# A hybrid decoder step on one Trainium2 core: x kept in a place of its own, rows broadcast in one pass, and the opening's loads and chunk quarters dealt anew

## The chip, the cores and the metric

The kernel runs on one core of one Trainium2 chip. The metric is device time of one execution in microseconds (us), lower is better. The core has a matrix engine (PE, TensorE), a vector engine (DVE, VectorE), an activation engine (ACT, ScalarE), a general engine (POOL, GpSimd) and a queue engine (SP, SyncE) that here does nothing but ask for loads. All of them run their own instruction lists in parallel and meet only at semaphores.

## What is computed

One step of a one-layer decoder trunk in float32, for a prompt of 256 tokens and for 8 sequences of 4 tokens, 288 token columns in all. Cut to what matters here:

```python
mod = silu(c) @ ada_w + ada_b                    # 9 conditioning rows, ada_w is 2048 x 12288
sh1, sc1, g1, sh2, sc2, g2 = split(mod, 6)
h = rms_norm(x) * (1 + sc1) + sh1
proj = h @ w_in                                  # 2048 x 18448, then HGRN2 and mLSTM heads
x = x + g1 * (merged @ w_out)
h = rms_norm(x) * (1 + sc2) + sh2
up = h @ w_up;  x = x + g2 * ((gelu(conv(a)) * g) @ w_down)
y = rms_norm(x, final_norm_w)
```

The mLSTM heads (8 of them) need, for each head, one row of running values (`-m_t`, exponents and so on) under every one of 128 partitions: a broadcast.

## The kernel before

Every large product is made from "chunks": a chunk is 512 rows by 256 columns of a weight matrix, loaded as 512 KB into a ring of four buffers `raw`. ACT rounds it to a high part `whi` (helper `hi(N, k)`), DVE makes the low part `wlo = raw - whi` (helper `lo(N, k)`), and PE then makes 24 matmuls of 288 columns (`whi` by the high part of h, `whi` by its low part, `wlo` by the high part; lines L770 to L772, in `pieces`). A quarter of a chunk, 6 matmuls, is called a piece. 584 chunks pass through the kernel.

The opening is different from the rest. h cannot be made before the first 4096 columns of `mod` are known, and these come from 32 MB of `ada_w`. They are made by eight "units" (`unit(u, tiles)` on PE), each of four halves h; a half is two loads of 512 KB and 8 matmuls of 512 columns (L903). When a unit's four halves are done, ACT copies the sums out (`unit(u)` on ACT, to `urows`), PE turns them (`unit_turn(u)`), and DVE adds the groups. Each two units give four more rows of h. So that PE has work between the halves, the first 18 chunks (`EARLY`), each of which needs only a part of h, are dealt among the halves of units 2 to 7: 8 pieces before unit 2, then `EARLY_PIECES[4 * (u - 2) + h]` pieces behind half h of unit u, and the remaining pieces, up to 72, behind unit 7. The sums of chunks 0 to 5 are copied to `SQ` by ACT (`to_padded`), those of later chunks are added by DVE (`early_add`); either frees one of two accumulator banks, which the chunk two later needs.

ACT and DVE walk through the same deal. Behind half h of unit u come the chunks that end there:

```python
for n in chunk_ends(u, h):
    early_chunk(n)      # evict or add chunk n, then hi / lo of chunk n + 4
```

and on ACT `unit(u)`, the copy of unit u's sums, stands ahead of the chunks of half 3. The order is fixed when the program is built; nothing is chosen at run time.

SP asks for loads in one fixed order: the eight loads of a unit, and between them chunks 4 and up, as many as `loads_ahead(u, c)` says ahead of load c of unit u. A unit's load waits until the same half of the unit before is used (`u_used`); a chunk's load waits for `lo_done` of the chunk four earlier. What is left of the first 20 chunks is asked for behind unit 7's last load.

x, turned to columns (`xT`), lies at the start of the memory that `SQ` takes later. Before the first sums may be copied to `SQ`, POOL writes `xT` to DRAM (`xT_spill`, 2 writes of 1152 KB), waits for that, and clears the padding columns of `SQ` (`hg["pad"]`).

The mLSTM broadcast is one matmul per head, `mm(R[:, 0, 0:EM + TS], ones8[:, :], mLR[:, :])`, of a float32 block of 8 rows by 360 columns; `rows_of(h)` on DVE fills `mLR` from `LR`, keeping row h alone. The gate rows of the mLSTM (`gate_rows`) are made on ACT and DVE beside the chunks 18 to 25, from q = 18 (`EARLY`) on.

Of the kernel before, what the change touches and what calls it, by code (L numbers as in the profile page):

```python
# [174 lines left out]
EARLY_PIECES = (1, 2, 1, 2, 2, 2, 1, 2, 2, 1, 3, 3, 3, 3, 3, 3, 3, 3, 3, 3, 3, 2, 2, 2)  # L175
# [84 lines left out]
def build(nc, x_prompt, x_sample, c_prompt, c_sample, state_hgrn, state_mlstm_C, state_mlstm_n, state_mlstm_m,  # L260
# [5 lines left out]
    with ExitStack() as ctx:  # L266
# [54 lines left out]
        ones8 = sb("ones8", [MH, P], stack=mixer)  # L321
# [21 lines left out]
        ctm = sb("ctm", [P, 2, P], stack=setup)  # L343
        cvr = sb("cvr", [2 * FT, NS, P], stack=setup)
        partm = sb("partm", [P, 4, P], stack=setup)
# [6 lines left out]
        ssx = sb("ssx", [P, 3], stack=setup)  # L352
# [33 lines left out]
        mLR = sb("mLR", [MH, EM + TS], stack=ml_mem)  # L386
# [358 lines left out]
        def _(pe):  # L745
# [499 lines left out]
        def _(act):  # L1245
# [434 lines left out]
        def _(dve):  # L1680
# [123 lines left out]
            def early_chunk(n):  # L1804
# [3 lines left out]
                if n + RING < EARLY + LEAD:  # L1808
                    lo(N_HG, n + RING)
# [365 lines left out]
        def _(pool):  # L2175
# [14 lines left out]
            cst_(nc.gpsimd.memset(ones8[:, :], 1.0))  # L2190
# [34 lines left out]
            pool.dma_start(cvr[:, :, :], state_conv[0].rearrange("b j (t c) -> (j t) b c", c=P)).then_inc(ld_conv, 16)  # L2225
            pool.wait_ge(x_c, KT + X_FREE)
            pool.wait_ge(u_used, 4 * BESIDE)
            for half in range(2):
                pool.dma_start(xT_spill[:, half * KT * T // 2:(half + 1) * KT * T // 2],
                               xT[:, 8 * half:8 * half + 8, :].rearrange("p a b -> p (a b)")).then_inc(ml["st"], 16)  # L2230

            pool.wait_ge(ml["st"], 32)
            pool.wait_ge(xn_done, 4)
            nc.gpsimd.memset(SQ[:, :, :, TP:TPAD].rearrange("p a b t -> p (a b) t"), 0.0).then_inc(hg["pad"], 1)
            pool.wait_ge(u_used, 4 * UNITS - 1)
            with nc.allow_non_contiguous_dma(reason="a few columns"):
# [243 lines left out]
```

## Time and profile before

| | |
|---|---|
| three runs, us | 2230.81, 2230.97 (median), 2234.35 |
| the profiled execution, its time | 2232.91 us |
| its span in the profile | 2231.2 us |
| PE busy | 2179.2 us, 98% of the span |
| DVE, ACT, POOL busy | 1143.9, 984.5, 362.1 us |
| DMA | 460.03 MB moved |

The profile gives, for each engine, when each instruction started, how long it took, and for idle time ahead of it what it waited for. Matmul records overlap, since the engine is pipelined: the time from one start to the next says what a matmul costs, not the length of its record. Times inside the kernel are counted from the start of the span.

### The profile page before, as it was taken

The page shows a single profiled execution, that of the slowest core. Times are in us where ns is not written, and L with a number is a line of the kernel's source. Part 1 is how long each engine was busy: PE and PEld are TensorE (multiplying, and loading weights), DVE is VectorE, ACT ScalarE, POOL GpSimd, SP SyncE. Part 2 cuts the span into 40 slices and gives each one's busy share as a digit, 9 for nine tenths or more (in the row PEclk, how much of TensorE's full clock was granted, in tenths as well). Part 3 has the DMA queues.
Part 4 walks back from the last instruction along what each step waited for, and adds up shares of the span by engine and source line. Part 5 has one row for each costly group of instructions (what it writes and reads, how often), then busy time and mean ns, then how long its engine had stood idle before and what let it go on. Part 6 is the DMA issues. An engine that isn't in the chain of part 4 may idle for free. (4 is left out here: it accounts for less than half of the span.)

```text
span 2231.2 us, 42202 instructions
## 1 busy us (share of the span) xinstructions
PE 2179.2 (98%) x17218; PEld 2057.1 (92%) x17218; DVE 1143.9 (51%) x1597; ACT 984.5 (44%) x1365; POOL 362.1 (16%) x525
## 2 busy tenths in 40 slices
PE   6899999999999999999999998999999999999997
PEld 3589999999999999999999987999999999999997
DVE  3356465564565544444445466555555555444443
ACT  3336563564454344454535335434444444433332
POOL 2000322332222331121212240000000000110000
PEclk9999999999999999999999999999999999999999
DMA  9987666666675767668676698555555555555553
GB/s 351 376 283 216 203 197 206 209 199 211 208 226 188 235 190 233 197 211 257 210 222 202 200 311 266 163 167 163 166 167 159 170 161 161 181 161 174 173 168 106
DMA packets 407411, 460.03 MB, mean 206 GB/s; under 512 B 14843, under 2 KB 379955, under 8 KB 406433
## 3 DMA queue, kind: packets, MB, share of 16 engines
q1 hardware_dynamic: 394192, 410.64, 58.8%
q0 software_dynamic: 12240, 46.03, 6.4%
q8 instruction: 109, 1.79, 0.3%
q10 hardware_dynamic: 833, 1.26, 0.2%
q14 instruction: 37, 0.30, 0.0%
HBM read 431.48 MB, written 26.39 MB: 205 GB/s over the span
## 5 line engine op out<-in xcount | busy, mean ns | idle before, releaser
L770 PE MATMUL ps<-xh,whi 128*128 128x288 f32 x3968 | 1190.0, 300 | 14.2 <-issue 7.2
L1689 DVE TENSOR_TENSOR wlo<-raw,whi 128x1024 fp32r<-128x1024 f32 x584 | 739.8, 1267 | 896.9 <-ACT whi L1256 894.8
L772 PE MATMUL ps<-xh,wlo 128*128 128x288 f32 x3968 | 1173.0, 296 | 0.0
L771 PE MATMUL ps<-xl,whi 128*128 128x288 f32 x3968 | 1172.8, 296 | 0.0
L1256 ACT ACTIVATE whi<-raw 128x1024 fp32r<-128x1024 f32 x584 | 616.6, 1057 | 756.3 <-PE ps L772 708.3
L770 PEld LDWEIGHTS ps<-xh,whi 128*128 128x128 f32 x3968 | 747.5, 188 | 54.8 <-issue 40.2
L771 PEld LDWEIGHTS ps<-xl,whi 128*128 128x128 f32 x3968 | 747.5, 188 | 0.7
L772 PEld LDWEIGHTS ps<-xh,wlo 128*128 128x128 f32 x3968 | 747.1, 188 | 0.0
L770 PE MATMUL ps<-ffh,whi 128*128 128x288 f32 x704 | 208.5, 296 | 0.0
L772 PE MATMUL ps<-ffh,wlo 128*128 128x288 f32 x704 | 208.0, 295 | 0.0
L771 PE MATMUL ps<-ffl,whi 128*128 128x288 f32 x704 | 207.9, 295 | 0.0
L770 PEld LDWEIGHTS ps<-ffh,whi 128*128 128x128 f32 x704 | 132.5, 188 | 0.3
L772 PEld LDWEIGHTS ps<-ffh,wlo 128*128 128x128 f32 x704 | 132.2, 188 | 0.0
L771 PEld LDWEIGHTS ps<-ffl,whi 128*128 128x128 f32 x704 | 132.1, 188 | 0.0
L2430 POOL COPY tails<-abuf 128x4 f32 x22 | 4.1, 188 | 419.1 <-ACT abuf L1624 419.1
L2320 POOL TENSOR_TENSOR S<-S,AC 128x1024 f32<-128x1024 f32 x16 | 32.3, 2019 | 133.1 <-PE R L1033 133.1
L2315 POOL TENSOR_TENSOR VM<-Vt,smask 128x1024 fp32r<-128x1024 f32 x16 | 35.4, 2211 | 85.9 <-issue 81.7
L1630 ACT ACTIVATE ffh<-yb 128x576 f32 (+1 forms) x22 | 15.1, 686 | 69.7 <-DVE yb L2110 69.7
L2103 DVE SCALAR_TENSOR_TENSOR acv<-abuf,par,acv 128x304 f32<-128x304 f32 x88 | 41.1, 529 | 0.0
L2425 POOL COPY abuf<-cst 128x16 f32 x44 | 21.2, 513 | 99.6 <-DVE acv L2103 91.0
L1259 ACT ACTIVATE arows<-ab 128x256 f32<-128x256 f32 x26 | 10.0, 383 | 60.2 <-PE ab L796 58.4
L796 PE MATMUL ab<-araw,cs 128*32 128x256 f32 x544 | 36.4, 385 | 0.0
(423 smaller groups left out, 1631.3 us busy)
## 6 DMA issues: line engine op xcount, KB each, us to landing
raw<-in_w_in SPq DMA_DIRECT2D x288, 512.0 KB, 4.7
raw<-in_w_up SPq DMA_DIRECT2D x176, 512.0 KB, 3.6
raw<-in_w_down SPq DMA_DIRECT2D x88, 512.0 KB, 3.5
araw<-in_ada_w SPq DMA_DIRECT2D x74, 512.0 KB, 6.0
uraw_x<-in_ada_w SPq DMA_DIRECT2D x36, 512.0 KB, 10.1
raw<-in_w_out SPq DMA_DIRECT2D x32, 512.0 KB, 3.5
top<-in_ada_w SPq DMA_DIRECT2D x24, 512.0 KB, 8.1
afill<-in_ada_w SPq DMA_DIRECT2D x18, 512.0 KB, 7.4
```

Of the source, the lines that this page charges most:

```text
L770: mm(o, whi[:, s, kk, cols], hi[:, kt0 + kk, :], start=first and kk == 0, stop=False)
L771: mm(o, whi[:, s, kk, cols], lo[:, kt0 + kk, :], start=False, stop=False)
L772: x = mm(o, wlo[:, s, kk, cols], hi[:, kt0 + kk, :], start=False, stop=last and kk == KC - 1)
L796: x = mm(acc[32 * kk:32 * kk + 32, 0:CN], cs[:, kt0 + kk, :], weights[:, kk, :], start=first, stop=last)
L1256: A(whi[:, s], raw[:, s], ACT.Copy).then_inc(hi_done, 1)
L1259: A(arows0[:, :], acc[:, 0:CN], ACT.Copy).then_inc(ada_rows, 1)
L1630: A(ffh[:, bass.ds(2 * i, 2), :], yb[:, :, :], ACT.Copy).then_inc(ff_hi, 1)
L1689: TT(wlo[:, s], raw[:, s], whi[:, s].bitcast(F32), ALU.subtract).then_inc(lo_done, 1)
L2103: STT(acv[:, m, 0:AB - 2], abuf[:, m, w:w + AB - 2], cw[w][:, c1], acv[:, m, 0:AB - 2], ALU.mult, ALU.add).then_inc(ff_conv, 1)
L2315: G(VM[:, :, :], mid(Vt[:, 2, :], NS), rep_last(smask8[:, :, :].rearrange("p a b -> p (a b)"), P), ALU.mult).then_inc(hg["vm"], 1)
L2320: G(S0[:, :, :], S0[:, :, :], rep_last(AC[:, 3, j, :], P), ALU.mult).then_inc(hg["scaled"], 1)
L2425: x = nc.gpsimd.tensor_copy(seq(abuf[:, m, 2 + TP:AB], 2 + LS)[:, :, 0:2], cst[:, bass.ds(2 * i + m, 1), :].rearrange("p o (b j) -> p (o b ...
```

## The change

Five edits come together.

1. `xT` moves to a place behind `reset8`, where nothing of the opening takes over its memory. The memory under `SQ` now holds only what dies early (masks, `ctm`, `partm`, `ssx`). The clearing of `SQ`'s padding waits for `xn_done` 1 in place of the write of `xT` and `xn_done` 4, and the write of `xT` itself moves from behind unit 1 to behind the gate weights' loads, which begin once half 1 of unit 7 is used. The gate rows (q = 22) now wait for that write on ACT and DVE.
2. The broadcast's rows become rounded ones: `mLR` is 128 rows high, cleared once, with the rounded row in rows 0 to 7 and what rounding left off in rows 32 to 39, and the matmul takes 128 rows by 360 columns of type float32r. DVE makes one more operation a head.
3. `loads_ahead` becomes a table, `LOADS_BESIDE`, by unit and load.
4. `EARLY_PIECES` gets other numbers.
5. Behind the first chunks ACT and DVE no longer take chunk n + 4 at once: for n = 1 to 6 they take chunk n + 3, and at n = 6 both, so that one copy of sums more stands ahead of each rounding.

```diff
-EARLY_PIECES = (1, 2, 1, 2, 2, 2, 1, 2, 2, 1, 3, 3, 3, 3, 3, 3, 3, 3, 3, 3, 3, 2, 2, 2)
+EARLY_PIECES = (3, 1, 0, 1, 1, 3, 1, 1, 3, 4, 4, 3, 3, 5, 1, 0, 5, 5, 5, 0, 3, 4, 1, 0)
+LOADS_BESIDE = (4, 4, 4, 4, 5, 5, 5, 5,
+                5, 6, 6, 6, 6, 6, 6, 6,
+                6, 6, 7, 7, 7, 7, 8, 8,
+                9, 10, 10, 10, 11, 11, 11, 11,
+                11, 11, 12, 13, 14, 14, 14, 15,
+                15, 15, 16, 16, 16, 17, 17, 17)
...
-    return RING if u == BESIDE else min(EARLY_LOADS, 2 * RING + pieces_ahead(u - 1, c // 2) // 4 - 2)
+    return LOADS_BESIDE[UC * (u - BESIDE) + c]
...
-        mLR = sb("mLR", [MH, EM + TS], stack=ml_mem)
+        mLR = sb("mLR", [P, EM + TS], F32R, stack=ml_mem)
...
-                    mm(R[:, 0, 0:EM + TS], ones8[:, :], mLR[:, :], start=True, stop=True).then_inc(ml["bc"], 1)
+                    mm(R[:, 0, 0:EM + TS], ones_r[:, :], mLR[:, :], start=True, stop=True).then_inc(ml["bc"], 1)
...
                     if n == 0:
-                        act.wait_ge(ml["st"], 32)
                         act.wait_ge(hg["pad"], 1)
                     act.wait_ge(used, n + 1 + FREE)
                     to_padded(early_tile(n), n % 2)
-                if n + RING < EARLY + LEAD:
+                if 0 < n <= 6:
+                    hi(N_HG, n + RING - 1)
+                if n >= 6 and n + RING < EARLY + LEAD:
                     hi(N_HG, n + RING)
...
+                if isinstance(h, int) and h:
+                    dve.wait_ge(ml["bc"], h)
+                TSC(mLR[0:MH, :], LR[:, 0:EM + TS], ident[0:MH, bass.ds(h, 1)], None, ALU.mult).then_inc(ml["lr"], 1)
+                dve.wait_ge(ml["lr"], 2 * h + 1)
+                STT(mLR[32:32 + MH, :], LR[:, 0:EM + TS], ident[0:MH, bass.ds(h, 1)], mLR[0:MH, :].bitcast(F32), ALU.mult, ALU.subtract).then_inc(ml["lr"], 1)
...
+            pool.dma_start(cvr[:, :, :], state_conv[0].rearrange("b j (t c) -> (j t) b c", c=P)).then_inc(ld_conv, 16)
+            pool.wait_ge(xn_done, 1)
+            nc.gpsimd.memset(SQ[:, :, :, TP:TPAD].rearrange("p a b t -> p (a b) t"), 0.0).then_inc(hg["pad"], 1)
+            pool.wait_ge(small_c, 5)
+            pool.wait_ge(u_used, 4 * UNITS - 2)
```

ACT at the end of the opening, before: the chunks of unit 6 (`whi`), the copy of unit 6's sums (the first `urows`), the chunks of unit 7 and the copy of unit 7's sums. The first row is chunk 14's rounding.

```order
L1256 ACTIVATE whi<-raw 128x1024 [waits used,landed2]
L1256 ACTIVATE whi<-raw 128x1024 [waits used,landed3]
L1317 ACTIVATE urows<-R 128x512 [waits ada_cols,u_used]
L1256 ACTIVATE whi<-raw 128x1024 [waits used,landed0]
L1256 ACTIVATE whi<-raw 128x1024 [waits used,landed1]
L1256 ACTIVATE whi<-raw 128x1024 [waits used,landed2]
L1317 ACTIVATE urows<-R 128x512 [waits ada_cols,u_used]
```

The same place of the changed kernel, again from chunk 14's rounding on.

```order
L1267 ACTIVATE whi<-raw 128x1024 [waits used,landed2]
L1267 ACTIVATE whi<-raw 128x1024 [waits used,landed3]
L1267 ACTIVATE whi<-raw 128x1024 [waits used,landed0]
L1267 ACTIVATE whi<-raw 128x1024 [waits used,landed1]
L1328 ACTIVATE urows<-R 128x512 [waits ada_cols,u_used]
L1267 ACTIVATE whi<-raw 128x1024 [waits used,landed2]
L1267 ACTIVATE whi<-raw 128x1024 [waits used,landed3]
L1328 ACTIVATE urows<-R 128x512 [waits ada_cols,u_used]
```

Before, the copy of unit 6's sums stood behind the rounding of chunk 15; now it stands behind that of chunk 17 (`landed1`).

SP at the same place, before: the tail of its list, from load 2 of unit 7 on. `uraw_x` and `uraw_a` are unit loads, `raw` are chunks; the last row is chunks 18, 19 and 20.

```order
L651 DMA uraw_x<-in_ada_w 128x2x512 [waits u_used] x2
L619 DMA raw<-in_w_in 128x4x256 [waits lo_done]
L651 DMA uraw_x<-in_ada_w 128x2x512 [waits u_used] x2
L651 DMA uraw_a<-in_ada_w 128x2x512 [waits u_used] x2
L619 DMA raw<-in_w_in 128x4x256 [waits lo_done] x3
```

And in the changed kernel, from loads 2 to 4 of unit 7 on; the last row is chunks 17, 18, 19 and 20.

```order
L662 DMA uraw_x<-in_ada_w 128x2x512 [waits u_used] x3
L630 DMA raw<-in_w_in 128x4x256 [waits lo_done]
L662 DMA uraw_x<-in_ada_w 128x2x512 [waits u_used]
L662 DMA uraw_a<-in_ada_w 128x2x512 [waits u_used] x2
L630 DMA raw<-in_w_in 128x4x256 [waits lo_done] x4
```

Chunk 17 was asked for ahead of load 4 of unit 7 (the row of one `raw` between the unit loads); now it is asked for behind load 7.

ACT in the middle of the opening, before: chunk 8's rounding, the modulation of four more rows of h, the copy of chunk 5's sums (`SQ`), chunk 9's rounding, the copy of unit 4's sums, and the roundings of chunks 10, 11 and 12.

```order
L1256 ACTIVATE whi<-raw 128x1024 [waits used,landed0]
L1302 ACTIVATE merged<-merged,mod 128x256 [waits xn_done,ada_free]
L1302 ACTIVATE merged<-merged,mod 128x256 x3
L1308 ACTIVATE xh<-merged 128x1152 [waits md_s,md_p]
L1326 ACTIVATE SQ<-ps 128x2x256 [waits used]
L1327 ACTIVATE SQ<-ps 128x2x4x8
L1256 ACTIVATE whi<-raw 128x1024 [waits used,landed1]
L1317 ACTIVATE urows<-R 128x512 [waits ada_cols,u_used]
L1256 ACTIVATE whi<-raw 128x1024 [waits used,landed2]
L1332 ACTIVATE cst<-ab 128x8x44 [waits small_t]
L1256 ACTIVATE whi<-raw 128x1024 [waits used,landed3]
L1256 ACTIVATE whi<-raw 128x1024 [waits used,landed0]
```

The same place now, from the rounding of chunk 7 on.

```order
L1267 ACTIVATE whi<-raw 128x1024 [waits used,landed3]
L1337 ACTIVATE SQ<-ps 128x2x256 [waits used]
L1338 ACTIVATE SQ<-ps 128x2x4x8
L1267 ACTIVATE whi<-raw 128x1024 [waits used,landed0]
L1267 ACTIVATE whi<-raw 128x1024 [waits used,landed1]
L1267 ACTIVATE whi<-raw 128x1024 [waits used,landed2]
L1328 ACTIVATE urows<-R 128x512 [waits ada_cols,u_used]
L1267 ACTIVATE whi<-raw 128x1024 [waits used,landed3]
L1343 ACTIVATE cst<-ab 128x8x44 [waits small_t]
L1267 ACTIVATE whi<-raw 128x1024 [waits used,landed0]
```

The copy of unit 4's sums stood behind the rounding of chunk 9 (`landed1`); now it stands behind that of chunk 10 (`landed2`).

## Rows read from the trace of the kernel before

**Rows 1.** The page: span; DVE's low parts; median time from issue to landing.
```profile
span 2231.2 us, 42202 instructions
...
L1689 DVE TENSOR_TENSOR wlo<-raw,whi 128x1024 fp32r<-128x1024 f32 x584 | 739.8, 1267 | 896.9 <-ACT whi L1256 894.8
...
raw<-in_w_in SPq DMA_DIRECT2D x288, 512.0 KB, 4.7
raw<-in_w_up SPq DMA_DIRECT2D x176, 512.0 KB, 3.6
```

**Rows 2.** Stretches: us; busy PE, PEld, DVE, ACT, POOL (instructions); clock; DMA, GB/s.
```profile
40.00:50.00 10.00, 4.95 (x27) 4.95 (x28) 8.35 (x11) 6.08 (x8) 0.12 (x1) 0.66 1.03 407
120.00:130.00 10.00, 10.00 (x75) 6.99 (x75) 4.51 (x8) 3.60 (x4) 0.00 (x0) 1.00 1.06 375
```

**Rows 3.** Waits of PE, 0 to 300 us: us in total, times, longest.
```profile
PE R L903 <- DMA uraw_x<-in_ada_w: 5.7, 4, 3.7
PE ps L770 <- DVE xl L1756: 5.3, 1, 5.3
PE ps L770 <- issue: 3.8, 3, 1.9
```

**Rows 4.** Timeline, 50 to 70 us: start, us, engine line operation, idle before it.
```profile
50.76 1.38 POOL L2234 MEMSET SQ<- 128x1536 f32 x1 [10.64 <-DMA xT_spill<-xT]
...
53.00 1.06 PE L903 MATMUL R<-uraw_x,cs 128*32 128x512 f32 x8
...
60.93 1.06 ACT L1256 ACTIVATE whi<-raw 128x1024 fp32r<-128x1024 f32 x1 [7.99 <-DMA raw<-in_w_in]
61.89 0.58 ACT L1326 ACTIVATE SQ<-ps 128x512 f32<-128x512 f32 x1
...
62.68 0.37 PE L770 MATMUL ps<-xh,whi 128*128 128x288 f32 x1 [1.86 <-issue]
...
68.23 1.60 PE L903 MATMUL R<-uraw_x,cs 128*32 128x512 f32 x8 [3.73 <-DMA uraw_x<-in_ada_w]
```

**Rows 5.** Timeline of PE: later waits for unit loads, and the start of chunk 18.
```profile
84.70 1.07 PE L903 MATMUL R<-uraw_x,cs 128*32 128x512 f32 x8 [0.86 <-DMA uraw_x<-in_ada_w]
...
87.39 1.06 PE L903 MATMUL R<-uraw_x,cs 128*32 128x512 f32 x8 [0.63 <-DMA uraw_x<-in_ada_w]
...
131.85 1.06 PE L903 MATMUL R<-uraw_x,cs 128*32 128x512 f32 x8 [0.46 <-DMA uraw_x<-in_ada_w]
...
146.01 0.37 PE L770 MATMUL ps<-xh,whi 128*128 128x288 f32 x1 [0.53 <-issue]
```

**Rows 6.** Timeline of PE: a turn and a piece; a unit half, three pieces, a unit half.
```profile
110.84 0.66 PE L749 MATMUL R<-ident,urows 128*128 128x128 f32 x4
...
111.26 0.38 PE L770 MATMUL ps<-xh,whi 128*128 128x288 f32 x1
...
113.82 1.07 PE L903 MATMUL R<-uraw_x,cs 128*32 128x512 f32 x8
...
114.81 0.40 PE L770 MATMUL ps<-xh,whi 128*128 128x288 f32 x1
...
117.40 1.06 PE L903 MATMUL R<-uraw_x,cs 128*32 128x512 f32 x8
```

**Rows 7.** Timeline: DVE's sum of a unit, DVE's addition of a chunk, ACT's copy of a unit.
```profile
111.92 0.30 DVE L1704 TENSOR_REDUCE msum<-R 128x36 f32<-128x144 f32 x1
...
117.07 0.68 DVE L1800 TENSOR_TENSOR SQ<-SQ,ps 128x512 f32<-128x512 f32 x1
...
122.11 0.60 ACT L1317 ACTIVATE urows<-R 128x512 f32<-128x512 f32 x1 [0.40 <-PE R L903]
```

**Rows 8.** Timeline of PE at the first of the eight broadcasts.
```profile
829.83 0.29 PE L772 MATMUL ps<-xh,wlo 128*128 128x288 f32 x1
830.06 0.87 PE L1053 MATMUL R<-mLR,ones 8*128 8x360 f32 x2
830.86 0.44 PE L749 MATMUL R<-ident,mWQ 128*128 128x128 f32 x2
```

More of the change, by code:

```diff
@@ L333, in build @@
         EM = T + TS + NS
-        xT = sb("xT", [P, KT, T], stack=setup)
+        below = ExitStack()
+        maskf = sb("maskf", [P, P], stack=below)
+        maskf_s = sb("maskf_s", [P, P], stack=below)
+        ctm = sb("ctm", [P, 2, P], stack=below)
+        partm = sb("partm", [P, 4, P], stack=below)
+        ssx = sb("ssx", [P, 3], stack=below)
+        below.close()
+        sb("below_sums", [P, 3 * 4 * TPAD], stack=setup)
         urows = sb("urows", [P, 2, UN], stack=setup)
-        maskf = sb("maskf", [P, P], stack=setup)
-        maskf_s = sb("maskf_s", [P, P], stack=setup)
         tokens = ExitStack()
@@ L342, in build @@
         uraw_x = sb("uraw_x", [P, UX, 2, UN], stack=setup)
[L343 to L345 removed]
+        convs = ExitStack()
+        cvr = sb("cvr", [2 * FT, NS, P], stack=convs)
+        convs.close()
         gw = sb("gw", [P, KT, GP], stack=setup)
@@ L1807, in early_chunk @@
                     early_add(n)
-                if n + RING < EARLY + LEAD:
+                if 0 < n <= 6:
+                    lo(N_HG, n + RING - 1)
+                if n >= 6 and n + RING < EARLY + LEAD:
                     lo(N_HG, n + RING)
@@ L2189, in _ @@
             cst_(nc.gpsimd.memset(ones[:, :], 1.0))
-            cst_(nc.gpsimd.memset(ones8[:, :], 1.0))
+            cst_(nc.gpsimd.tensor_copy(ones_r[:, :], ones[:, :]))
             cst_(nc.gpsimd.memset(epsc[:, :], EPS))
@@ L2221, in _ @@
             cst_(G(smask[:, :], smask[:, :], rows[:, 0, 3], ALU.add))
+            pool.dma_start(cvr[:, :, :], state_conv[0].rearrange("b j (t c) -> (j t) b c", c=P)).then_inc(ld_conv, 16)
[3 more added lines that the diff above has]
+            pool.wait_ge(u_used, 4 * UNITS - 2)
             cst_(nc.gpsimd.memset(gw[:, :, MH:32], 0.0))
             assert cnt[0] == CONST_ALL
[L2225 to L2235, printed above, removed]
             with nc.allow_non_contiguous_dma(reason="a few columns"):
@@ L2241, in _ @@
                 pool.dma_start(m0[:, :], state_mlstm_m[0].rearrange("b h -> h b")).then_inc(ld_gs, 16)
+            pool.wait_ge(x_c, KT + X_FREE)
+            for half in range(2):
+                pool.dma_start(xT_spill[:, half * KT * T // 2:(half + 1) * KT * T // 2],
+                               xT[:, 8 * half:8 * half + 8, :].rearrange("p a b -> p (a b)")).then_inc(ml["st"], 16)
             pool.wait_ge(row_d, ROW_WK)
@@ L2382, in _ @@
             pool.wait_ge(hg["st"], 32 * (HH + 1))
-            for a in (dx[:, TPAD:4 * P], mQz[:, :, :]):
+            for a in (mLR[:, :].bitcast(F32), dx[:, TPAD:4 * P], mQz[:, :, :]):
                 nc.gpsimd.memset(a, 0.0).then_inc(ml["zero"], 1)
             nc.gpsimd.memset(mV[:, :, MV:MV + 1], 1.0).then_inc(ml["zero"], 1)
-            pool.wait_ge(ml["zero"], 3)
+            pool.wait_ge(ml["zero"], 4)
             for i in range(0, 3):
```

12 lines of the change are left out of this document (7 added, 5 removed).

## The prediction

> **What bounds the kernel now.** I read the page first, then the stretches, then PE's waits, then the timeline of the first 150 us. PE is busy 98% of the span, so an edit pays only where PE waits or where it takes PE time away. In the stretch 120 to 130 us PE starts 75 matmuls in 10 us, 0.133 us each [rows 2]: nothing can be hidden behind PE there, and a piece of 6 matmuls costs 0.8 us. The DMA engines are full there as well (1.06 busy, 375 GB/s) and at 40 to 50 us (1.03, 407 GB/s) [rows 2], so the opening is a race of two full resources. PE's waits in it [rows 3 to 5]:
> - 5.3 us until the first low part of h is there. No edit touches it.
> - 1.86 us at 62.68. ACT waited 7.99 us for chunk 4 to land, rounded it at 60.93, and only then, at 61.89, copied the sums of chunk 1, whose bank PE needed for chunk 3 [rows 4]. An instruction that waits holds back all behind it.
> - 3.73 us at 68.23 for the first loads of unit 3, with the clock low after it: these 8 matmuls take 1.60 us, those at 53.00 take 1.06 [rows 4].
> - 0.86, 0.63 and 0.46 us for loads, and 0.53 us at chunk 18 [rows 5].
>
> Without the first, that is 8.1 us, with the low clock about 9. It is the most that a better opening can win.
>
> The Trainium skill (TensorE: Matmul & The Clock Gate, Architectural detail) says that ACT and DVE are strict FIFO. The trace agrees with it at 60.93 and 61.89; it is the rule that speaks against the new deal. If ACT could pass a rounding that waits, the waits found below at turns 3, 4 and 6 would be nothing, and the change would win.
>
> **The change part by part.**
>
> *One-pass rows.* From the start of the broadcast to the next instruction is 0.80 us, for 360 columns in two records [rows 8]. A rounded matmul of 288 columns costs 0.133 [rows 2], so 360 columns should cost 0.17. Eight heads: 8 x 0.63 = 5.0 us at most. The step from the rounded matmuls into the broadcast takes 0.23 (829.83 to 830.06) and not 0.133 [rows 8]; if such a 0.1 is now paid on the way out, or twice, 4.2 or 3.4 is left. I take 4.6, nearer to the upper end, since the same step is saved on the way in. Nothing hides it, PE being the bound there. DVE's second operation a head is hidden in its idle half. The Trainium skill (FP8 and Floating Point Precision) gives true float32 four passes; by it one pass would save three quarters of 0.80, also 4.8 in eight.
>
> *xT's place.* Its write is 2304 KB, at 375 GB/s 6.3 us of the full DMA, ahead of unit 2's second load; the `SQ` memset waited for it until 50.76 [rows 4]. Both leave the opening. It comes back from about 148 us on, where chunks have four buffers and DMA has slack. I take 0.3 us, 0 to 3 for the range.
>
> *Loads and pieces.* Now the race has to be walked again. Prices: unit half 1.0, plus 0.2 where pieces stand ahead of it (113.82 to 114.81, and three pieces to 117.40); turn 0.4 (110.84 to 111.26) [rows 6]; piece 0.8. A unit load takes the DMA 1.35 us (84.70 to 87.39 are two). From 68.23 to 131.85, 63.6 us, 36 unit loads and 10 chunks land, so a chunk takes (63.6 - 48.4) / 10 = 1.5 [rows 4, 5]. A load that finds the DMA empty takes 3.6 to 4.7 [rows 1]. ACT rounds in 1.06, DVE in 1.27, and a unit's copy takes 0.60 [rows 1, 4, 7].
>
> Unit 2 begins at 53.0 as before. The bank for chunk 3 is free in time (ACT copies chunk 1 ahead of rounding chunk 4), so the 1.86 is gone. Load 1 of unit 3 may be asked for at 54.0, when half 0 of unit 2 is used; load 0 takes 3.6, chunk 5 and load 1 come behind it: 60.5, not 68.2, before PE needs it at 61.6 (from 53.0: four halves 4.0, five pieces 4.0, three switches 0.6). So the 3.73 is gone too. Then:
> - Unit 3 (six pieces, a turn, 10.0 in all) ends at 71.6, half 0 of unit 4 at 72.8. Behind chunk 3, ACT now stands at the rounding of chunk 6, ahead of the copy of unit 3. Chunk 6 is asked for in unit 4's row: 8 unit loads and itself behind 60.5, landing 72.8. Plus 1.06, 0.60 and 0.1 of semaphores the turn can start at 74.6: **wait 1.8.**
> - 14 pieces, 3 halves, a turn and small transposes: half 0 of unit 5 ends at 91.9. The copy of unit 4 is behind the rounding of chunk 10, landing 92.4 (10 unit loads, 4 chunks later). Turn at 94.2: **wait 2.3.**
> - A turn, 7 pieces and a half later, at 101.4, PE comes to the first piece of chunk 10, whose bank DVE frees by adding chunk 8. That stands behind the low part of chunk 11, asked for in unit 6's row (6 unit loads and itself behind chunk 10), landing 102.0. Plus 1.06, 1.27, and DVE's sum of unit 4 and the addition of chunk 8 (0.5 and 0.9, of which 0.30 and 0.68 are the rows' larger halves) [rows 7]: 105.8. **Wait 4.4.**
> - The rest of unit 5 takes 4.5, unit 6 (15 pieces, a turn, four halves) 17.0: it ends near 127.7 with bank waits of 0.4, with no piece behind its last half. The copy of its sums is behind the rounding of chunk 17, and chunk 17 is asked for behind loads 6 and 7 of unit 7, which wait for that very half. So 3.6 + 1.35 + 1.5 + 1.06 + 0.60 + 0.1 = 8.2 us pass, while PE has one half of unit 7 to do, 1.0: **wait 7.2.**
> - Unit 7 with 8 pieces takes 10.4 from there, to 146.3; the copy and turn 1.1; the 7 pieces left 5.6: chunk 18 at 153.0. Its low parts and rows of h come in time, so the 0.53 is not repeated.
>
> Clock: the stretch 40 to 50 us, which holds the idle of 5.3, was granted 0.66 [rows 2, 3]: the lower level (1.2 GHz) for 6.8 of its ten us. At least 1.5 of these fell on work, at most all, so the idle cost 0.8 to 3.4 us more. I take 1.7 behind the 7.2, 1.3 behind the 4.4, and nothing behind the shorter ones (behind 0.5 to 0.9 us the matmuls of [rows 5] take 1.06 as ever): 3.0, and 0 to 5 for the range.
>
> **The sum.** Chunk 18 starts at 153.0 + 3.0 = 156.0 against 146.0 [rows 5]: +10.0. Rows -4.6, the write +0.3: **+5.7 us.** Made against the profiled execution (span 2231.2, its time 2232.91), it gives 2238.6; on the median of the three runs, 2230.97, it is 2236.7, which I forecast, since those are what will be compared. A difference of 0.2%, 4.5 us, is about what can be told from none here.
>
> **Rivals.**
> - *The two sides cancel.* Loads behind an almost empty queue land sooner (chunk 17 in the 3.6 of a single load: wait 4.4 in place of 7.2), the low clock costs 1 and not 3, and the third wait is 3.0. Then the opening loses 3.8, the rows and the write give back 4.3, and it is 2230.5; with only one of the three, 2233.9 to 2235.3. For it: the rows show landings of single loads alone. Against: chunk 17's request is third in line. Chance 0.33, with all that ends within 0.2%.
> - *Faster.* ACT and DVE don't stand in PE's way: chunks land earlier than I count, because without the write the DMA runs ahead by 6 us of data. Then all of the 9 us are won, less the 4.4 that the order of requests forces: 9 - 4.4 + 4.6 = 9.2, 2221.8. It decides for faster if the waits at units 3 to 5 sum to under 3 us, where I have 8.5. Against: a unit load can't be asked for before the same half of the unit before is used, so the run-ahead ends after 8 loads. Chance 0.10.
> - *The rows don't do what they say*: the new matmul of 128 rows is no cheaper than 0.80: +10.3, 2241.3. Against: rounded matmuls of the same height start every 0.133 [rows 2]. Chance 0.05.
> - *The write collides*: at 148 to 160 us it halves the share of the chunks' loads, and PE waits 3 us more in all: +8.7, 2239.7. Chance 0.12.
>
> **Chances and range.** Slower by over 0.2%: my case 0.40, rows 0.05, collision 0.12, together 0.57. Within: 0.33. Faster: 0.10. The range: low end 2229 (the cancelling case, and past its best third only faster cases), high end 2242 (my case with the low clock at 5 and chunk 17 at 4.7, or rows that bring nothing).
>
> **What would show it.** In the changed kernel's trace: no wait of ACT for chunk 4 ahead of a copy to `SQ`, no wait at the start of unit 3; PE's turn 6 (L760 on `urows`) waiting about 7 us for ACT's `urows`, at about 129 us; a wait of 4 us for DVE's `SQ` about 101 us; two of about 2 us at turns 3 and 4; chunk 18 at 153 to 157; broadcasts 0.2 to 0.3 us from start to next. Wrong I would be if the wait at turn 6 were under 3 us, or if chunk 18 began before 148.

## The result, and the profile after

The changed kernel takes 2247.04 us (median of five runs, 2243.57 to 2247.81), the kernel before 2230.97 in runs beside it (2230.81 to 2234.35). The ratio, which is that of the means (2246.1 and 2232.0), is 1.0063, with a 95% interval of 1.0051 to 1.0074: slower by 11 to 17 us. The forecast was 2236.7, with 2242 as the upper end; the side was right, the size was not. The profiled execution took 2247.27 us.

The page of the changed kernel, span and busy time, and PE's waits up to 300 us (us in total, times, longest). [Rows 1, 3] answer to them.

```profile
span 2245.5 us, 42195 instructions
...
PE 2176.3 (97%) x17210; PEld 2061.3 (92%) x17210; DVE 1151.6 (51%) x1605; ACT 985.1 (44%) x1365; POOL 363.3 (16%) x526
```

```profile
PE R L760 <- ACT urows L1328: 11.5, 4, 7.6
PE R L760 <- issue: 6.7, 1, 6.7
PE ps L781 <- issue: 5.8, 2, 4.4
PE ps L781 <- DVE xl L1769: 5.3, 1, 5.3
PE ps L914 <- DMA uraw<-in_ada_w: 5.1, 3, 3.0
PE ab L760 <- ACT ctm L1274: 3.5, 1, 3.5
PE R L981 <- DVE gwl L1875: 2.5, 1, 2.5
PE R L914 <- DMA uraw_x<-in_ada_w: 1.2, 2, 0.6
```

PE's waits for unit loads fell from 5.7 us [rows 3] to 1.2, and in their place stand 11.5 us for ACT's copies of unit sums and 4.4 us at chunk 10. L914 is the unit half (L903 before), L781 to L783 are the pieces, L760 the turns. The timeline of PE shows those at turn 4, chunk 10 and turn 6, the start of chunk 18 (at 146.01 before, [rows 5]) and the first gate matmul.

```profile
97.93 0.66 PE L760 MATMUL R<-ident,urows 128*128 128x128 f32 x4 [1.31 <-ACT urows L1328]
109.78 0.37 PE L781 MATMUL ps<-xh,whi 128*128 128x288 f32 x1 [4.42 <-issue]
...
141.48 1.11 PE L760 MATMUL R<-ident,urows 128*128 128x128 f32 x4 [7.57 <-ACT urows L1328]
...
159.99 0.37 PE L781 MATMUL ps<-xh,whi 128*128 128x288 f32 x1
...
167.89 0.32 PE L981 MATMUL R<-xh,gwh 128*40 128x288 f32 x1 [2.46 <-DVE gwl L1875]
```

So the opening ends 14.0 us late (159.99 - 146.01), and the gate matmuls 16.6 (before they began at 151.25). What ACT did ahead of 141.48 and of 167.89:

```profile
134.13 1.06 ACT L1267 ACTIVATE whi<-raw 128x1024 fp32r<-128x1024 f32 x1 [5.51 <-DMA raw<-in_w_in]
139.89 1.06 ACT L1267 ACTIVATE whi<-raw 128x1024 fp32r<-128x1024 f32 x1 [4.70 <-DMA raw<-in_w_in]
140.85 0.58 ACT L1328 ACTIVATE urows<-R 128x512 f32<-128x512 f32 x1
...
164.79 1.06 ACT L1267 ACTIVATE whi<-raw 128x1024 fp32r<-128x1024 f32 x1 [3.09 <-DMA raw<-in_w_in]
165.75 0.72 ACT L1396 ACTIVATE gwh<-gw 128x640 fp32r<-128x640 f32 x1
```

Twice a copy that needs nothing but ACT stands behind a rounding that waits for a load. And SP, the engine that asks for loads, with the time of each request:

```profile
43.75 0.37 SPq L630 DMA_DIRECT2D raw<-in_w_in  x1
44.16 1.02 SPq L662 DMA_DIRECT2D uraw_x<-in_ada_w  x2
45.22 0.98 SPq L662 DMA_DIRECT2D uraw_a<-in_ada_w  x2
56.74 0.37 SPq L662 DMA_DIRECT2D uraw_x<-in_ada_w  x1
```

Between 46.2 and 56.7 us nothing is asked for: the next row of SP's list waits for half 0 of unit 2. The stretches show what that does (clock, then DMA's busy share and GB/s at the end of each row). The kernel before:

```profile
50.00:70.00 20.00, 14.41 (x101) 8.79 (x100) 6.66 (x10) 5.34 (x10) 1.38 (x1) 0.97 1.06 377
70.00:90.00 20.00, 18.52 (x128) 12.30 (x128) 6.53 (x10) 8.80 (x15) 0.00 (x0) 0.95 1.06 378
90.00:110.00 20.00, 20.00 (x154) 14.82 (x157) 7.46 (x13) 5.38 (x7) 0.00 (x0) 1.00 1.06 377
110.00:130.00 20.00, 20.00 (x149) 14.15 (x143) 10.68 (x19) 9.13 (x12) 0.00 (x0) 1.00 1.06 376
130.00:150.00 20.00, 18.84 (x145) 15.94 (x147) 12.62 (x21) 9.23 (x14) 4.00 (x5) 1.00 1.02 290
```

The changed kernel:

```profile
50.00:70.00 20.00, 19.33 (x137) 13.61 (x136) 7.49 (x13) 4.63 (x9) 0.00 (x0) 0.95 0.80 283
70.00:90.00 20.00, 17.47 (x117) 12.32 (x116) 5.88 (x8) 8.92 (x15) 0.00 (x0) 0.91 1.06 375
90.00:110.00 20.00, 14.27 (x108) 10.98 (x107) 6.57 (x12) 5.27 (x6) 0.00 (x0) 1.00 1.05 372
110.00:130.00 20.00, 19.85 (x136) 13.78 (x136) 9.57 (x16) 7.81 (x11) 0.00 (x0) 0.91 0.80 274
130.00:150.00 20.00, 12.43 (x86) 9.66 (x84) 6.33 (x11) 3.65 (x4) 2.78 (x4) 0.83 0.71 233
```

Before, DMA is full from 50 to 130 us. After, it is partly idle at 50 to 60 us (0.55 busy, 183 GB/s), at 110 to 120 (0.57, 187) and at 140 to 150 (0.41, 122). From 50 to 70 us PE itself is ahead of before (19.33 busy, not 14.41): it is later that it pays. The mean over these 100 us falls from 360 to 307 GB/s: 5.2 MB less have come by 150 us, and at the 377 GB/s of a full DMA that is 13.9 us, about the delay of chunk 18. This is the delay counted a second time, and not yet its cause: an opening that is late has loaded less by a given time, whatever made it late. Here are the same 100 us before, in the change, and in a run told below, where every request stands as in the change and two rows are exchanged on ACT:

```profile
50.00:150.00 100.00, 91.78 (x668) 66.00 (x670) 43.95 (x73) 37.89 (x56) 5.39 (x6) 0.98 1.05 359
```

```profile
50.00:150.00 100.00, 83.36 (x576) 60.34 (x574) 35.85 (x58) 30.28 (x44) 2.78 (x4) 0.92 0.88 307
```

```profile
50.00:150.00 100.00, 87.86 (x620) 62.69 (x620) 37.36 (x63) 33.04 (x48) 5.50 (x8) 0.96 0.95 327
```

2.0 MB of the 5.2 are back without a change of any load. Part of the idle DMA is made by PE and ACT waiting, and only the runs can say what the requests themselves cost.

The broadcast, to be read beside [rows 8]:

```profile
848.13 0.29 PE L783 MATMUL ps<-xh,wlo 128*128 128x288 f32 x1
848.26 0.33 PE L1064 MATMUL R<-mLR,ones_r 128*128 128x360 f32 x1
848.43 0.38 PE L760 MATMUL R<-ident,mWQ 128*128 128x128 f32 x2
```

It costs 0.17 in place of 0.80, and the step into it 0.13 in place of 0.23: 0.73 by these rows.

### The profile page after: what moved, and what is told of

Its sections match the earlier page's. It is cut to its first block and busy times, and to the rows that moved or that the text cites. A ratio compares the mean times of both kernels' runs of the same rounds, so it can differ in the third digit from the quotient of the medians.

```text
span 2245.5 us, 42195 instructions
## 1 busy us (share of the span) xinstructions
PE 2176.3 (97%) x17210; PEld 2061.3 (92%) x17210; DVE 1151.6 (51%) x1605; ACT 985.1 (44%) x1365; POOL 363.3 (16%) x526
## 5 line engine op out<-in xcount | busy, mean ns | idle before, releaser
L781 PE MATMUL ps<-xh,whi 128*128 128x288 f32 x3968 | 1192.4, 301 | 16.7 <-issue 9.5
L783 PE MATMUL ps<-xh,wlo 128*128 128x288 f32 x3968 | 1175.4, 296 | 0.0
L781 PEld LDWEIGHTS ps<-xh,whi 128*128 128x128 f32 x3968 | 749.8, 189 | 56.0 <-issue 41.9
L783 PEld LDWEIGHTS ps<-xh,wlo 128*128 128x128 f32 x3968 | 749.3, 189 | 0.0
L781 PE MATMUL ps<-ffh,whi 128*128 128x288 f32 x704 | 208.5, 296 | 0.0
L783 PE MATMUL ps<-ffh,wlo 128*128 128x288 f32 x704 | 208.0, 295 | 0.0
L781 PEld LDWEIGHTS ps<-ffh,whi 128*128 128x128 f32 x704 | 132.5, 188 | 0.3
L783 PEld LDWEIGHTS ps<-ffh,wlo 128*128 128x128 f32 x704 | 132.2, 188 | 0.0
```

Source lines behind the costliest of these rows:

```text
L781: mm(o, whi[:, s, kk, cols], hi[:, kt0 + kk, :], start=first and kk == 0, stop=False)
L783: x = mm(o, wlo[:, s, kk, cols], hi[:, kt0 + kk, :], start=False, stop=last and kk == KC - 1)
```

## The experiments

Each kernel was timed in rounds beside the kernel before, whose median was 2232.7 to 2232.9 us in all of them but that of the change (2230.97), so it is the ratios that are compared. Differences between two runs are told from their ratios, and where the two intervals overlap they are not clear of noise by themselves. Before has chunk 18 at 146.01.

| kernel | median us | ratio (95%) | chunk 18 starts |
|---|---|---|---|
| the change | 2247.04 | 1.0063 (1.0051 to 1.0074) | 159.99 |
| rows alone | 2228.61 | 0.9978 (0.9968 to 0.9988) | 146.38 |
| the three deal edits undone | 2227.66 | 0.9977 (0.9967 to 0.9987) | 144.74 |
| the same, early write | 2229.07 | 0.9986 (0.9977 to 0.9995) | 146.76 |
| new order alone kept of the deal | 2228.14 | 0.9978 (0.9969 to 0.9987) | 141.63 |
| and new pieces | 2230.29 | 0.9992 (0.9983 to 1.0001) | 146.54 |
| and unit 7's row of loads | 2237.65 | 1.0031 (1.0019 to 1.0043) | 150.95 |
| change, rows of units 3 and 4 undone | 2243.49 | 1.0047 (1.0033 to 1.0061) | 158.44 |
| change, chunk 17 asked for sooner | 2238.73 | 1.0023 (1.0014 to 1.0032) | 151.07 |
| change, copy ahead of chunk 17 on ACT | 2238.07 | 1.0025 (1.0016 to 1.0034) | 152.81 |
| change, early write | 2244.15 | 1.0049 (1.0035 to 1.0062) | 159.56 |
| change, later write | 2242.94 | 1.0041 (1.0027 to 1.0055) | 160.82 |
| order, later write (the best) | 2224.09 | 0.9965 (0.9952 to 0.9977) | 141.97 |

**The rows by themselves.** The kernel before with edit 2 and nothing else.

```diff
-        mLR = sb("mLR", [MH, EM + TS], stack=ml_mem)
+        mLR = sb("mLR", [P, EM + TS], F32R, stack=ml_mem)
-  mm(R[:, 0, 0:EM + TS], ones8[:, :], mLR[:, :], start=True, stop=True)
+  mm(R[:, 0, 0:EM + TS], ones_r[:, :], mLR[:, :], start=True, stop=True)
```

> The kernel before with the one-pass rows alone (mLR 128 rows high and rounded, second DVE operation a head); nothing of the opening is touched. Theory A (what the trace after shows): a broadcast falls from 0.80 to about 0.15 us and each of the eight heads is 0.78 us shorter, 6.2 us in all: 2225 against 2231. Rival B (the prediction's term): 4.6 us, 2226.4. Rival C: the gain is lost again at the later heads, where the trace after gives back 1.5 to 2.3 us between 1207 and 1257 us, because DVE's second operation is late there: the saving is 4 us or less and PE's waits for mWQ and mod grow by 1.5 us as they did in the changed kernel. If those waits grow only when the opening is changed too, C is wrong.

Measured: 2228.61; by the ratio 2.7 to 7.1 us less, 4.9 in the middle. Each head gains 0.78: the first four broadcasts stand at 830.06, 891.90, 956.02 and 1017.88 us before, at 831.82, 892.89, 956.24 and 1017.30 here. But at one head PE waits for DVE after the broadcast, and there nothing is won. Before, and then with the rows:

```profile
1218.10 0.96 PE L749 MATMUL R<-ident,mWQ 128*128 128x128 f32 x7 [1.63 <-DVE mWQ L1964]
```

```profile
1215.27 0.95 PE L749 MATMUL R<-ident,mWQ 128*128 128x128 f32 x7 [2.42 <-DVE mWQ L1968]
```

The wait grew by 0.79, all that the head had saved: 8 x 0.78 - 0.8 = 5.4 by the trace. Its span is only 4.1 shorter, because it already stands 1.76 late at the first broadcast, with the opening untouched: 0.37 at chunk 18, and 1.39 more behind it. In both traces PE waits 1.43 us at about 234 us; behind that wait the clock was granted 1.00 before and 0.67 here (the third number from the end):

```profile
235.00:240.00 5.00, 5.00 (x40) 5.00 (x39) 1.23 (x1) 4.10 (x4) 3.41 (x5) 1.00 0.36 105
```

```profile
233.98 0.37 PE L770 MATMUL ps<-xh,whi 128*128 128x288 f32 x1 [1.43 <-issue]
```

```profile
235.00:240.00 5.00, 5.00 (x29) 5.00 (x28) 0.14 (x1) 2.60 (x3) 2.90 (x6) 0.67 0.39 108
```

So the wait that C names does grow with the opening untouched, but by 0.79 us and not by 1.5 (PE's longest wait for `mod` grows too, from 1.11 to 1.80, and costs nothing: the two traces stand 3.62 us apart ahead of it and behind it). A's 6.2 was read off ahead of the wait for `mWQ`. The interval of 2.7 to 7.1 holds A, B and the upper end of C alike; it is the trace that tells them apart.

**The deal undone.** The changed kernel with the old pieces, rule of loads and order.

```diff
-EARLY_PIECES = (3, 1, 0, 1, 1, 3, 1, 1, 3, 4, 4, 3, 3, 5, 1, 0, 5, 5, 5, 0, 3, 4, 1, 0)
+EARLY_PIECES = (1, 2, 1, 2, 2, 2, 1, 2, 2, 1, 3, 3, 3, 3, 3, 3, 3, 3, 3, 3, 3, 2, 2, 2)
-    return LOADS_BESIDE[UC * (u - BESIDE) + c]
+    return RING if u == BESIDE else min(EARLY_LOADS, 2 * RING + pieces_ahead(u - 1, c // 2) // 4 - 2)
-                if 0 < n <= 6:
-                    hi(N_HG, n + RING - 1)
-                if n >= 6 and n + RING < EARLY + LEAD:
+                if n + RING < EARLY + LEAD:
```

> The changed kernel with three of its edits undone: the old EARLY_PIECES, the old rule for the loads, the old order of sums and rounding. What is left: xT's place, the late write, the one-pass rows. Theory A: the new deal makes the waits at turns 3, 4, chunk 10 and turn 6 (about 15 us with the low clock behind them), so chunk 18 starts at about 146 or before, and since the unit loads are no longer behind the write the 3.7 us wait at unit 3 shrinks: 2221 to 2226. Rival B: the lost 14 us at chunk 18 come from xT's place and the early padding (the start at 46.6 in place of 45.1 us and the DMA that ran dry at 50 to 60 us): then chunk 18 still starts 5 us or more late and the time is above 2230. Both keep the late write, so the wait of 2.5 us at the gate rows and the late chunk 21 should be here too if the write makes them.

Measured: 2227.66, 5.1 us less than before by the ratio. The median lies 1.7 us above A's range and short of B's 2230. A's cause holds: the ratio is that of the rows alone (0.9977 and 0.9978), so the loss is in the three deal edits. Chunk 18 starts 1.3 us ahead of before even with a first piece 1.7 us later, which B excludes. The late write shows at the gates: PE waits 1.3 us there, and not at all with the early write of the next run. Ahead of chunk 18 it waits 2.0 us, and 0.5 with the early write; but the order run below, which writes late too, waits only 0.65 there, so this part is not shown to be the write's.

**The write asked for early**, in the changed kernel and in the one with the deal undone, by the same edit.

```diff
+            pool.wait_ge(x_c, KT + X_FREE)
+            pool.wait_ge(u_used, 4 * BESIDE)
+            (the two writes of xT to xT_spill, here and no longer behind the gate weights)
             pool.wait_ge(small_c, 5)
             pool.wait_ge(u_used, 4 * UNITS - 2)
```

> The changed kernel with the write of xT asked for at its old place in time (once unit 1 is used), still waited for only at the gate rows. Theory A: the late write, 2304 KB beside chunks 20 to 23, makes chunk 21 land late, ACT's rounding of it waits 3.1 us and holds the copy of the gate weights, and PE waits 2.5 us with a low clock behind: 4.3 us from chunk 18 to the end of the gates' stage. Here that goes: the gates' stage loses nothing, and as the DMA is only 0.4 to 0.7 busy from 50 to 60 us the write costs 0 to 2 us there: 2243 to 2245 against 2247. Rival B: chunk 21 is late because chunks 18 to 21 are asked for late (behind the late unit 7), not because of the write: the gates' wait stays and the time is 2247 to 2250. Rival C: the write at 52 us delays unit 3 by its 6 us and the time is 2249 or more.

> The old deal (old pieces, loads and order) with xT's place and the one-pass rows, and with the write of xT asked for once unit 1 is used, waited for only at the gate rows. Theory A: the late write collides with chunks 18 to 21 (in the same kernel with the late write ACT waited 6.9 us for the landing of chunk 19's turn at 133.3 us, PE 2.0 us ahead of chunk 18 and 1.3 us at the gates); early, it brings back the wait of 3.7 us at unit 3 but DMA has then 80 us to make it good: 2224 to 2227 against 2227.7, and PE's waits between 130 and 160 us fall from 6.5 to about 2 us. Rival B: the opening is bound by DMA throughout, so the 6 us of the write cost the same wherever they stand ahead of 150 us: 2227 to 2229.

Measured: 2244.15 with the new deal, and the wait at the gates is 0.2 us, so A (the ratio falls by 3.1 us, but the two intervals overlap; it is the trace that shows it). With the old deal 2229.07, the end of rival B's range: there DMA is full, a wait of 3.1 us at unit 3 came back, and between early and late (0.9986 and 0.9977) there is no difference clear of noise.

**Chunk 17 sooner, or no longer in the way.** Two kernels. In the first only the last row of the table changes; in the second only ACT's list, with every load as it was.

```diff
-                15, 15, 16, 16, 16, 17, 17, 17)
+                15, 15, 16, 16, 18, 18, 18, 18)
```

```diff
+                    ends = list(chunk_ends(u, h))
+                    if u == 6 and h == 2:
+                        ends.pop()
                     if h == 3:
                         unit(u)
-                    for n in chunk_ends(u, h):
+                    if u == 6 and h == 3:
+                        early_chunk(chunk_ends(6, 2)[-1])
+                    for n in ends:
```

> The changed kernel with chunks 16 and 17 asked for ahead of load 4 of unit 7 in place of load 5, and so ahead of the loads that wait for half 2 of unit 6. Theory A: the wait of 7.6 us at turn 6 is that of ACT's copy behind the rounding of chunk 17, which is asked for behind loads that wait for the very half; asked for sooner it lands 4 to 6 us sooner and 4 to 6 us of the wait go, with about 1 us of low clock: 2240 to 2243. Rival B: chunk 17's load waits for the low part of chunk 13, which is itself late, so SP stands there and loads 4 to 7 of unit 7 come later as well: the wait moves to unit 7's halves and the time is the same within 1.5 us, or longer.

> The changed kernel with two rows exchanged on ACT alone: the copy of unit 6's sums stands ahead of the rounding of chunk 17 in place of behind it. No load, piece or other row moves. Theory A (an instruction that waits holds back what is behind it): the wait of 7.6 us at turn 6 falls to about 0.7, the copy's own time; chunk 17 is needed only behind unit 7, and unit 7's loads follow the halves of unit 6, so most of it is kept: 6 to 8 us with the low clock behind the wait, 2239 to 2241. Rival B: chunk 17 and unit 7's loads land as late as ever and PE meets them a few us on: turn 6 falls, but waits for unit 7's halves or for chunk 17 grow by as much, and the time is 2244 to 2247.

Measured: 2238.73 and 2238.07, 8.9 and 8.5 us less than the change by their ratios, and both a little better than A's ranges. At turn 6 PE waits 1.17 and 0.89 us, not 7.57. Rival B's waits don't come: unit 7's halves wait for nothing in either run; a piece ahead of turn 6 waits, 1.37 and 1.12 us. ACT and PE in the second:

```profile
133.59 1.06 ACT L1267 ACTIVATE whi<-raw 128x1024 fp32r<-128x1024 f32 x1 [4.26 <-DMA raw<-in_w_in]
134.55 0.58 ACT L1328 ACTIVATE urows<-R 128x512 f32<-128x512 f32 x1
140.32 1.06 ACT L1267 ACTIVATE whi<-raw 128x1024 fp32r<-128x1024 f32 x1 [5.20 <-DMA raw<-in_w_in]
```

```profile
135.18 0.66 PE L760 MATMUL R<-ident,urows 128*128 128x128 f32 x4 [0.89 <-ACT urows L1328]
```

The wait of 7.57 us is 0.89, by two rows exchanged on an engine that is 44% busy. Chunk 17 still isn't rounded before 140.32, and PE doesn't need it until behind unit 7.

**Order, pieces, loads, one after the other.** From the deal undone, the new order is put back; then the new pieces; then the table's row of unit 7; and, from the other end, the change with its rows of units 3 and 4 undone.

```diff
 unit 7's row from the table, the rule's numbers above it:
+                14, 14, 15, 15, 15, 15, 15, 15,
                 15, 15, 16, 16, 16, 17, 17, 17)
 the rows of units 3 and 4 undone, in the change:
-                5, 6, 6, 6, 6, 6, 6, 6,
-                6, 6, 7, 7, 7, 7, 8, 8,
+                8, 8, 8, 8, 9, 9, 9, 9,
+                9, 9, 9, 9, 9, 9, 9, 9,
```

> The kernel with xT's place, late write, one-pass rows and the old pieces and loads, but with the new order of sums and rounding (for n = 1 to 6 chunk n + 3, then n + 4). Theory A: the order by itself costs nothing, since every sum copied stands behind a rounding that waits one chunk less; time 2226 to 2229, as with the old order (2227.7). Rival B: from n = 6 on both roundings come at once, and the rounding of chunk 10 is as late as in the changed kernel, so the wait at chunk 10 (4.4 us there) appears with the old tables too: 2230 to 2233.

> The changed kernel with its table of loads undone: the old rule for the loads, the new pieces, the new order, the late write. Theory A: the table is what lets DMA run dry (0.66 and 0.43 busy at 50 to 60 us) and puts chunks 6, 10, 11 and 17 late; with the old rule the waits at turns 3, 4 and 6 and at chunk 10 are under 2 us each and 6 to 12 us of the 15 come back: 2232 to 2240. Rival B: the pieces themselves do it: chunks are needed sooner than DMA can bring them whatever the order of requests, so the waits move to unit loads behind chunks, and the time stays at 2243 or more.

> The changed kernel with the rows of units 3 to 6 of its table put back to the old rule, and the row of unit 7 alone as in the change: chunk 17 asked for ahead of load 5 of unit 7, as before this edit of mine. Theory A: the wait at chunk 10 (4.1 us with units 3 and 4 put back) belongs to the rows of units 5 and 6 and goes; that at turn 6 belongs to unit 7's row and stays at 6 to 8 us: 2236 to 2239. Rival B: the wait at turn 6 is what is left of a DMA queue that is late from unit 5 on, so with the rows of units 5 and 6 put back it falls under 3 us and the time is that of the old rule throughout, 2230 to 2233.

> The changed kernel with the rows of units 3 and 4 alone put back in its table of loads: 8 chunks ahead of unit 3 and 9 from its load 4 on, in place of 5 to 6 and 6 to 8. Units 5 to 7, so chunk 17 too, as in the change. Theory A: the table costs in two places. The waits at turn 3 (1.9), turn 4 (1.3) and chunk 10 (4.4) and the dry DMA at 50 to 60 us belong to these rows, and go, 6 to 8 us; the wait at turn 6 of 7.6 us belongs to the last row, and stays, since chunk 17 is asked for behind loads that wait for half 2 of unit 6: 2238 to 2241, with turn 6 waiting 6 to 8 us. Rival B: all chunks ahead come sooner, so chunk 17 as well, and the wait at turn 6 shrinks below 4 us: 2232 to 2236. Rival C: the late requests were no loss of DMA time overall and the waits only move to the unit loads: 2244 or more.

Measured: 2228.14, 2230.29, 2237.65, 2243.49. The order costs nothing that can be measured. The pieces cost 3 us (0.9978 to 0.9992; the intervals overlap), and with them and the rule the time is below what A of that run gave; PE then waits at neither turn 3, turn 4 nor chunk 10, and 2.40 us at turn 6. The table is the loss: 0.9992 to 1.0063, 16 us, clear of noise. Unit 7's row alone makes 9 of them (0.9992 to 1.0031), with 7.34 us at turn 6: A.

The rows of units 3 and 4 make 3.6 (1.0063 to 1.0047; the intervals overlap) and not 6 to 8, and the time lies above A's range, near C's: the waits at turns 3 and 4 went to none and 0.95, but 4.1 us stayed at chunk 10, and the waits for unit loads grew from 1.2 to 2.3. DMA was full again at 50 to 60 us (1.01 busy, not 0.55), so its idle time there is a small part of the loss at most; here A was wrong. With the rows of units 5 and 6 at the rule's numbers too, PE doesn't wait at chunk 10, so that wait belongs to them: the last 3.6 us (1.0047 to 1.0031; the intervals overlap).

**The write later.** In the order run the rounding of chunk 21 (not 20, as the expectation has it) waited 3.47 us for its load, and the gates 2.2. One line more:

```diff
             pool.wait_ge(x_c, KT + X_FREE)
+            pool.wait_ge(lo_done, 22)
             for half in range(2):
```

> Old pieces and loads, new order, xT's place and one-pass rows as in the run of the order, with one wait more: the write of xT is asked for once the low part of chunk 21 is made, some 17 us later. In that run DMA was full until 155 us and 0.39, 0.18 and 0.26 busy from 155 to 170, chunk 18's rounding waited 6.5 us, chunk 20's 3.5 us and the gate matmuls 2.2 us. Theory A: the write is what holds them; later it is free, PE's wait of 2.2 us at the gates goes and the waits between 125 and 150 us shrink by 1 to 2 us more: 2223.5 to 2226 against 2228.1, and 2225.5 is my number. Rival B: DMA is full there because the chunks were asked for late, the write only fills the rest: under 1 us is won. Rival C: the write is now too late for the gate rows, which wait for it on ACT and DVE from 165 us on and hold the roundings behind them: 2228 or more.

> The changed kernel with the write of xT asked for once the low part of chunk 21 is made. Up to 150 us it is the changed kernel, row for row, so it is a second look at its opening too. Theory A: the gate matmuls no longer wait (2.5 us with low clock behind, 3 to 4 us in all), 2242 to 2244; and the first piece starts anywhere from 45.0 to 47.7 us, as over the runs so far whatever their opening holds, with chunk 18 at 157 to 160. Rival B: the late first piece (46.6) and the low clock up to it belong to the change, so they are here too, at 46.4 to 46.8; the gates' wait goes as well. Rival C: chunk 21 is late in this opening because its load waits for the low part of chunk 17, which is late, not because of the write: the gate matmuls wait over 1.5 us still, and the time is 2245 or more.

Measured: 2224.09 with the old deal, 0.35% below the kernel before and the lowest of all; 2242.94 with the new one. Both times are in A's ranges, and the waits at the gates are gone (none, and 0.17). By the ratios the later write is worth 2.9 and 4.9 us; the intervals overlap, and the traces show what went. What A said of the waits between 125 and 150 us did not come: chunk 18's rounding waited 6.5 us as before, and only what stands behind the write's place got sooner. ACT in the first, where the copy for the gates now meets no late load:

```profile
141.54 1.06 ACT L1261 ACTIVATE whi<-raw 128x1024 fp32r<-128x1024 f32 x1 [0.71 <-PE ps L777]
142.50 0.72 ACT L1390 ACTIVATE gwh<-gw 128x640 fp32r<-128x640 f32 x1
```

The second is the change up to 150 us, and a second look at its opening:

```profile
45.10 0.61 PE L781 MATMUL ps<-xh,whi 128*128 128x288 f32 x1 [5.33 <-DVE xl L1769]
...
141.26 1.11 PE L760 MATMUL R<-ident,urows 128*128 128x128 f32 x4 [8.09 <-ACT urows L1328]
```

The first piece is at 45.10, not at 46.61 as in the trace of the change, yet turn 6 is at 141.26 and chunk 18 at 160.82, as late as there and 0.8 us beyond A's 157 to 160.

## Why the prediction was wrong

The side and the waits were right, the sum was 5.7 where the profiled spans differ by 14.3. Two terms failed. The start of chunk 18 was forecast at +10.0 and came at +14.0, from a start of unit 2 taken as that of before, two waits left out and a low clock priced too low. And the write was put at +0.3, because "DMA has slack" there, and came at +4.3. Term by term:

- **The 1.86 and 3.73 us are gone**: right, and the waits for loads at units 3 and 4 shrank to 0.55 and 0.60.
- **The waits at turns 3, 4, chunk 10 and turn 6** were forecast at 1.8, 2.3, 4.4 and 7.2 and came at 1.92, 1.31, 4.42 and 7.57: 15.7 forecast, 15.2 measured. The exchange on ACT shows turn 6's cause by experiment. For the others the load rows show that late requests make them; that the copy stood behind the waiting rounding there too is read from the trace. The Trainium skill (TensorE: Matmul & The Clock Gate, Architectural detail) has ACT and DVE take their instructions strictly in order; the exchange, 7.57 to 0.89 us, agrees.
- **"Chunk 18 starts at 153.0 + 3.0 = 156.0"**: the step that failed first, by 4.0 us. "Unit 2 begins at 53.0 as before" was one part: in this trace it began at 55.61, since the first piece began 1.56 later, and its matmuls started every 0.24 us until 51.8 (before, until 48.1) and every 0.13 only then. The two waits for loads that were left, 1.15 together, were another, and the low clock of the next item the third. Against the trace before, the 14.0 are 2.6 of later start, 8.9 more of PE's waits from unit 2 to chunk 18 (17.1 against 8.2), and 2.5 that are left, which I take for the low clock between. The late start is not what decides: in the second look unit 2 began at 54.18, the waits were 16.6, and chunk 18 came as late, with a clock of 0.90 from unit 2 to chunk 18 in place of 0.93. Why the clock differed between the two was not tested.
- **The low clock, 3.0 us**, was too small. The granted clock was 0.72 at 80 to 85, 0.66 at 110 to 115 and 0.58 at 140 to 145 us, behind the waits of 1.9, 4.4 and 7.6 us. (1 - clock) x 5 gives 1.4, 1.7 and 2.1; less what PE idled of the last, 4.5 to 5.2. I had put nothing behind the shorter waits. (153.0 + 2.6 + 1.15 - 0.5 + 4.5 is 160.8 for the measured 160.0, so the work between the waits was priced about 0.8 us too high.)
- **The write, +0.3.** Measured +4.3: the first gate matmul is 16.6 late where chunk 18 was 14.0, and behind the gates it is 18.3 (848.13 against 829.83 ahead of the first broadcast, [rows 8]), from the 2.46 us of wait and the low clock behind it (0.81 at 165 to 170 us, 0.85 at 170 to 175). With the later write the wait is 0.17, and in the old deal it goes from 2.19 to none. I wrote that "DMA has slack" from 148 us on. The write itself took the slack: in the ten us around the gates DMA is 1.10 busy (160 to 170 us) where it was 0.71 before (150 to 160), and the gate weights' copy stood behind the rounding of chunk 21, which waited 3.09 us for its load. A late opening is not needed for it: the order run has chunk 18 at 141.63 and waits 2.19. The low clock behind is not sure to come: the run with the exchange on ACT waits 2.93 us there, and was granted 1.00 from 160 to 170 us. The collision was my own rival at +8.7, with a chance of 0.12 and a price of 3.
- **The rows, -4.6.** Measured 4.9 (2.7 to 7.1), and by the trace 5.4: near by luck, two errors that cancel in part. A head saves 0.78, not 0.57, and one head's saving is taken by DVE. In the trace of the change 1.5 more went there, between 1210 and 1240 us, where the clock fell to 0.94 behind the 2.4 us wait; with the deal undone, the same wait was followed by 1.00.

Together: 14.0 + 4.3 - 6.2 + 0.8 + 1.5 = 14.4, measured 14.3. Of the 8.6 that the forecast lacked, 4.0 are the opening's, 4.0 the write's, 0.7 the rows'.

What stays open: what fixes the start of the first piece. Over the traces it lies between 45.05 and 47.69 us, also where the opening is that of before (45.58) or of the change (46.61 and 45.10). PE is granted the low clock at different times in them (1.00 up to 40 us before, 0.50 from 35 to 50 in the change, 0.50 from 25 to 30 and again from 45 to 50 in the fastest run); no run was made on it. Open too is how the 16 us of the table would fall to its rows if they were undone in another order: each was undone in one setting only.

## What to carry to other kernels

Where two resources are both full, walk the schedule for each, and look also where the engine that asks for loads stands at a wait with little outstanding. But bytes missing at a given time only say how late the kernel is: here the rows with the idle DMA at 50 to 60 us were worth 3.6 us, and the last row of the table, with one chunk asked for behind loads that wait for a late half, was worth 9. A list of requests in one order that follows consumption closely ("ask as late as it still lands in time") has no reserve: one late half stops the requests, and they stop PE. And on an in-order engine, a short copy that frees the bottleneck belongs ahead of any instruction that waits for a transfer which nobody needs yet; here that exchange alone was worth 8.5 us, where eight matmuls at a fifth of their price gave 4.9.

## What the runs showed of the hardware

- The float32 broadcast, 8 rows by 360 columns, costs 0.80 us in two records and the rounded one with 128 rows 0.17, a factor of 4.7. The Trainium skill (FP8 and Floating Point Precision, Matmul Precision) counts four passes for true float32, which would leave 0.20; the rows decide, and with the step ahead of it a head gained 0.78.
- A write of 2304 KB that the gate matmuls don't wait for delayed the loads beside it so that PE waited at the gates: 2.46 us in the change, 2.19 in the order run, 2.42 in the pieces run, 1.3 to 2.9 over the eight kernels with the write there. Asked for earlier or later, 0 to 0.2 us.
- A wait of PE of the same length is not always followed by the same clock. Behind 1.43 us at about 234 us the next 5 us were granted 1.00 before and 0.67 with the rows alone; behind 2.4 us at about 1215 to 1232 us, 1.00 with the deal undone and, over 30 us, 0.94 in the change.
- The same opening, instruction for instruction, had the first matmul of its first piece at 46.61 and at 45.10 us in two executions, and ended at 159.99 and 160.82.
